# Sums of squares in one block behind two slabs of a linear, instead of a piece behind each chunk

## What is computed

```
x = x + gate * rmsnorm(y, g_post)          # y: output of the block before
h = rmsnorm(x, g_pre) * (1 + scale) + shift
next = h @ w_in                            # the next linear
```

## Time and profile before

| | us |
|---|---|
| median of 3 runs | 3676.74 |
| lowest, highest | 3656.36, 3680.42 |
| the profiled execution | 3671.71 |
| its span | 3669.9 |
| TensorE busy | 3312.0 (90%) |
| VectorE busy | 1804.5 (49%) |
| ScalarE busy | 1076.0 (29%) |
| GpSimd busy | 1045.9 (28%) |
| mean granted clock of TensorE | 0.925 of full |

### The profile page before, as it was taken

The page is one execution under the profiler, slowest core; times in us unless marked ns, Lnnn a source line. Parts: engine busy times, 40 slices in busy tenths (PEclk is TensorE's granted clock), DMA queues, the critical chain, the costliest instruction groups (busy, mean ns, idle before and its releaser), DMA issues.

```text
span 3669.9 us, 53161 instructions
## 1 busy us (share of the span) xinstructions
PE 3312.0 (90%) x17596; PEld 2645.3 (72%) x17600; DVE 1804.5 (49%) x3266; ACT 1076.0 (29%) x1919; POOL 1045.9 (28%) x563
## 2 busy tenths in 40 slices
PE   6789699999988898999988898999999678899997
PEld 4756588888876667998966556788778445578876
DVE  4665777753355664422436465433231366744323
ACT  2144232111131553322222132432231034543222
POOL 1111122323213102444423210444444111134443
PEclk9789899999999998999979795999999669999999
DMA  6101234433111001232211100232222100023222
GB/s 236 55 0 53 97 103 142 145 126 98 54 49 40 1 1 58 92 95 92 88 58 61 45 1 3 81 97 91 93 91 92 46 1 1 1 70 96 95 94 80
DMA packets 74335, 258.67 MB, mean 70 GB/s; under 512 B 9456, under 2 KB 12016, under 8 KB 72688
## 3 DMA queue, kind: packets, MB, share of 16 engines
q1 hardware_dynamic: 60256, 205.61, 17.5%
q10 hardware_dynamic: 13968, 51.65, 4.2%
HBM read 253.03 MB, written 2.10 MB: 70 GB/s over the span
## 4 chain that ended last, share of the span: by engine, by line
PE 81%; DVE 6%; issue 6%; ACT 3%; DVEq 1%; ACTq 1%; DMA 1%; SPq 0%; POOL 0%; POOLq 0%; PEldq 0%
PE ps L799 53%; PE ps L777 6%; PE ps L1995 5%; PE ps L2009 3%; PE ps L1190 2%; PE ps L1195 1%; PE ps L423 1%; PE ps L949 1%; PE ps L463 1%; PE ps L2189 1%; PE ps L2157 1%; DVE ps L400 1%; PE ps L2005 1%; PE ps L2151 1%; DVE rot_s L985 1%
## 5 line engine op out<-in xcount | busy, mean ns | idle before, releaser
L745 POOL TENSOR_TENSOR w_lo<-w_raw,w_hi 128x1024 fp32r<-128x1024 f32 (+1 forms) x373 | 918.3, 2465 | 1810.0 <-ACT w_hi L637 1810.0
L637 ACT ACTIVATE w_hi<-w_raw 128x1024 fp32r<-128x1024 f32 (+1 forms) x373 | 386.1, 1039 | 1284.7 <-PE ps L799 1039.5
L799 PE MATMUL ps<-h_hi,w_hi 128*128 128x258 f32 (+2 forms) x1824 | 321.1, 330 | 48.6 <-ACT w_hi L637 44.3
L799 PEld LDWEIGHTS ps<-h_hi,w_hi 128*128 128x128 f32 x1824 | 272.9, 195 | 82.5 <-issue 37.8
L799 PE MATMUL ps<-h_hi,w_lo 128*128 128x258 f32 (+2 forms) x1824 | 308.7, 321 | 0.0
L799 PE MATMUL ps<-h_lo,w_hi 128*128 128x258 f32 (+2 forms) x1824 | 307.9, 321 | 0.0
L799 PEld LDWEIGHTS ps<-h_hi,w_lo 128*128 128x128 f32 x1824 | 265.6, 190 | 27.7
L799 PEld LDWEIGHTS ps<-h_lo,w_hi 128*128 128x128 f32 x1824 | 264.5, 190 | 26.8
L1995 PE MATMUL ps<-keys,qs 128*128 128x256 f32 (+3 forms) x1008 | 225.3, 352 | 54.1 <-POOL qs L1158 48.2
L1995 PEld LDWEIGHTS ps<-keys,qs 128*128 128x128 f32 x1008 | 159.0, 201 | 117.1 <-issue 94.2
L1232 DVE TENSOR_REDUCE nm<-ps 128x1 f32<-128x512 f32 (+5 forms) x304 | 178.5, 587 | 112.1 <-PE ps L1997 51.9
(11 more groups left out here) (307 smaller groups left out, 5295.1 us busy)
## 6 DMA issues: line engine op xcount, KB each, us to landing
w_raw<-in_ffn_in SPq DMA_DIRECT2D x176, 512.0 KB, 3.6
mod_row<-in_w_mod_rows ACTq DMA_DIRECT2D x80, 512.0 KB, 4.5
w_raw<-in_ffn_out SPq DMA_DIRECT2D x64, 512.0 KB, 3.7
w_raw<-in_ev_in SPq DMA_DIRECT2D x26, 512.0 KB, 3.7
w_raw<-in_ffn_out SPq DMA_DIRECT2D x32, 384.0 KB, 3.1
w_raw<-in_od_in SPq DMA_DIRECT2D x21, 512.0 KB, 3.6
mod_ring<-in_w_mod SPq DMA_DIRECT2D x8, 1024.0 KB, 13.1
w_raw<-in_wo_in SPq DMA_DIRECT2D x12, 512.0 KB, 3.6
```

The costliest lines, as they stand in the source:

```text
L637: act.activation(k.w_hi[:, s, 0:self.KT * P], k.w_raw[:, s, 0:self.KT * P], ACT.Copy).then_inc(k.sems["w_hi_ready"], 1)
L745: ins = pool.tensor_tensor(k.w_lo[:, s, 0:self.KT * P], k.w_raw[:, s, 0:self.KT * P], k.w_hi[:, s, 0:self.KT * P].bitcast(F32), ALU.subtract)
L799: ins = pe.matmul(k.ps[:, 2 * s + g, 0:t1 - t0], w[:, s, c * P:(c + 1) * P], h[:, c, t0:t1], start=(n == 0), stop=(n == len(parts) - 1))
```

## The change

The sums of squares of all 8 chunks stand in one block behind the last matmul of the first two slabs. `n_sq` has 8 buffers instead of two, and the wait of ScalarE on `sq_used` and that semaphore are gone. `n_t` moves to another address, to make room. The number of instructions that compute is the same on every engine.

```diff
@@ class Gate
-        self.b = {... ("gate_x", DC), ("sq_ready", DC), ("sq_used", DC - 1))}
+        self.b = {... ("gate_x", DC), ("sq_ready", DC))}
@@ def pe_squares(self, pe, c):
         pe.wait_ge(k.sems["sq_ready"], self.b["sq_ready"] + c + 1)
         for i in range(self.T // P):
-            ins = pe.matmul(k.ps[:, 6, i:i + 1], k.n_sq[:, c % 2, i * P:(i + 1) * P], ...)
-        ins.then_inc(k.sems["sq_used"] if c < DC - 1 else k.sems["sums_ready"], 1)
+            ins = pe.matmul(k.ps[:, 6, i:i + 1], k.n_sq[:, c, i * P:(i + 1) * P], ...)
+        if c == DC - 1:
+            ins.then_inc(k.sems["sums_ready"], 1)
@@ def scalar(self, act, chain):
             self.pre.act_hi(act, c)
-            if c >= 2:
-
-                act.wait_ge(k.sems["sq_used"], b["sq_used"] + c - 1)
-            act.activation(k.n_sq[:, c % 2, :T], k.x[:, c, :T], ACT.Square).then_inc(k.sems["sq_ready"], 1)
+            act.activation(k.n_sq[:, c, :T], k.x[:, c, :T], ACT.Square).then_inc(k.sems["sq_ready"], 1)
@@ Linear.tensor, the first two slabs behind a Gate
             for c in range(K):
                 order += [hi_in(c), (0, 0, c), (0, 2, c), (1, 0, c), (1, 2, c)]
-                if isinstance(a, Gate):
-                    order.append(lambda c=c: a.pe_squares(pe, c))
                 order += [lo_in(c), (0, 1, c), (1, 1, c)]
             if isinstance(a, Gate):
+                order += [lambda c=c: a.pe_squares(pe, c) for c in range(K)]
                 order.append(lambda: self.norm.pe_spread(pe))
@@ memory
-    k.n_sq = at("n_sq", [P, 2, TOK], F32, A)
-    k.n_t = at("n_t", [P, 2, TOK], F32, A + 6144)
+    k.n_sq = at("n_sq", [P, DC, TOK], F32, A)
+    k.n_t = at("n_t", [P, 2, TOK], F32, A + 24576)
```

More of the change, by code:

```diff
@@ L448, in __init__ @@
         kit.stages[-2].feed()
-        self.b = {n: kit.reserve(n, c) for n, c in (("sums_ready", 1), ("std_ready", 1), ("rstd_ready", 1), ("rstd_spread", 1), ("gate_t", DC), ("gate_x", DC), ("sq_ready", DC), ("sq_used", DC - 1))}
+        self.b = {n: kit.reserve(n, c) for n, c in (("sums_ready", 1), ("std_ready", 1), ("rstd_ready", 1), ("rstd_spread", 1), ("gate_t", DC), ("gate_x", DC), ("sq_ready", DC))}
         self.pre = Pre(kit, norm_cols, shift, groups, hi, lo)
@@ L462, in pe_squares @@
         for i in range(self.T // P):
-            ins = pe.matmul(k.ps[:, 6, i:i + 1], k.n_sq[:, c % 2, i * P:(i + 1) * P], k.ones[:, 0:1], start=(c == 0 and i == 0), stop=(c == DC - 1), skip_group_check=True)
-        ins.then_inc(k.sems["sq_used"] if c < DC - 1 else k.sems["sums_ready"], 1)
+            ins = pe.matmul(k.ps[:, 6, i:i + 1], k.n_sq[:, c, i * P:(i + 1) * P], k.ones[:, 0:1], start=(c == 0 and i == 0), stop=(c == DC - 1), skip_group_check=True)
+        if c == DC - 1:
+            ins.then_inc(k.sems["sums_ready"], 1)
     def scalar(self, act, chain):
```

## The result

| | before | after |
|---|---|---|
| median, us | 3674.23 (4 runs) | 3712.78 (4 runs) |
| lowest, highest | 3656.36, 3680.42 | 3711.64, 3717.33 |
| the profiled execution, span | 3671.71, 3669.9 | 3717.33, 3715.5 |
| mean granted clock | 0.925 | 0.914 |

The change makes the kernel slower: ratio 1.0115, 95% interval 1.0079 to 1.0152. The ratio is formed from all executions; the quotient of the two medians is 1.0105. The forecast was 3712 us (3692 to 3729). The profiled execution of after is the slowest of its four, so the two traces differ by 45.6 us where the medians differ by 38.5.

A forecast was written before the change was run, and what follows sets the result against it. TensorE was taken as the bound, by only 0.27 us per chunk at G1. Slabs and blocks +34.7, spreads +4.6 and restarts +0.7 made +40.0 on the profiled 3671.7: 3712 us, range 3692 to 3729.

The forecast's parts named there:

- End of the slabs: First two slabs at G1 to G4: end 2.8, 2.7, 8.1 and 8.5 us before the old sums' end, 22.1 together.
- The sum: Whole kernel: 34.7 for slabs and blocks, 4.6 for spreads, 0.7 for restarts, +40.0 us on the profiled 3671.7.
- The block: Squares behind the slabs: full clock for 3.5 us, then half; 17.6 us for 96, 10.8 for 64, 56.8 in all.
- The rule weighed against it: In the four blocks, the skill's rule that gapless work keeps full clock: 37.4 us instead of 56.8; the forecast rejected it.
- The spreads: Behind each block, spreads start at half clock: +1.4 us at G1 and G2, +0.9 at G3 and G4, +4.6 together.
- The restart: The third slab's first matmuls behind the spread run more at half clock: +0.7 us, between 0 and +3.
- The other edits: ScalarE's missing wait, the other engines' work and the new addresses: no cost or gain beyond that counted in the loop's end.
- Rival 1: In the four blocks, full clock is kept to the end: +15.3 us, 3687 us; chance 0.09.
- rival 2: The loop can't keep full clock and TensorE enters the block at half: 3726 to 3742 us; chance 0.08.
- rival 3: In the four blocks, squares are cheaper alone, gaining below 0.069 us each; at 0.030, 3659 us; chance 0.03.
- rival 4: No effect: squares stay hidden, or gains at G3 and G4 balance the loss: 3665 to 3680 us; chance 0.02.

The follow-up runs named there:

- experiments 2 to 4: The changed kernel with the block at G3 and G4 only, at G1 and G2 only, or done twice: ratios to before 1.0005, 1.0095 and 1.0309.
- experiment 4: The changed kernel with every block of squares done twice, only the second pass signalling: 3780.03 us, 1.0309 of before.
- experiment 5: The changed kernel with 160 unused 512-column float32r matmuls among the squares in the blocks: 3726.37 us, 1.0161 of before.
- experiment 1: The changed kernel with the squares back between the chunks, keeping eight buffers, new addresses and no wait: 3665.54 us, 0.9992 of before.
- experiment 3: The changed kernel with the block at G1 and G2 only, squares between the chunks elsewhere: 3698.89 us, 1.0095 of before.

## Why the forecast was right, step by step

- *End of the slabs.* It holds to 0.1 us. From the second h_hi to the block's first weight load, which is where the slabs end, after takes 22.53, 22.54, 15.09 and 14.92 us at G1 to G4. Before took 25.33, 25.16, 23.12 and 23.54 to the end of the sums: 22.1 us less together, as forecast. The loops kept VectorE's pace, 3.21 and 2.14 us per chunk. That they do so at full clock, which the forecast assumed, held too: the clock was up by 451, 1069, 1475 and 1891.5, in each loop's first chunks. One reading was too wide: before, TensorE stood at half clock at G3 and G4 in the windows of the earlier trace rows, but from 1449.5 and 1862.5 on it had full clock. The sum doesn't use this, since it goes by the ends of the sums.
- *The block.* 16.2, 16.3, 9.5 and 11.4 us, 53.4 in all where the forecast had 56.8. The half-clock price, 0.2135 from start to start, holds. The full-clock price is 0.112, and the prediction's own rows say so (1.35/12 is 0.1125 and 3.65/32 is 0.114, not 0.117); this makes about 1 us of the 3.4. The rest is when the clock falls: 3.5 us after the block's start was taken, and it fell after 4.8, 4.7, 4.7 and 2.9. The mean of two blocks was a thin basis; its spread of +-1 us was inside the range. In the eight further blocks of experiments 2 to 4 the clock fell too, after 2.5 to 5.3 us.
- *The rule weighed against it.* Had the clock stayed full the blocks would have been 37.4 us long by the prediction's price. Measured 53.4, with TensorE busy in every window. The Trainium skill, TensorE: Matmul & The Clock Gate ("Why this matters for your kernels"), asks only to keep TensorE busy and free of idle gaps between bursts of matmuls. Here that was not enough to hold the clock: by experiment 4 a longer block doesn't bring it back, and by experiment 5 wide matmuls in between keep it.
- *The spreads.* 2.93, 2.93, 2.08 and 2.08 us, the +4.6 of the forecast.
- *The restart.* Mis-sized: +0.7 was taken within 0 to 3. The clock rose 5.2, 6.2, 6.1 and 3.2 us after the third slab's first matmul, where it was 2.8, 3.9, 5.3 and 3.0 before; 5.7 us more at half clock lose some 2.8. At G1 the first 16 matmuls take 5.41 us instead of 4.34.
- *The other edits.* Costed at nothing; experiment 1 shows nothing in its medians.
- *The sum.* Blocks 3.4 under, restarts 2.1 over: -22.1 + 53.4 + 4.6 + 2.8 gives +38.7, and the medians differ by 38.5. That it meets the medians to 0.2 us is luck, since before's four executions alone span 24; so is it that the forecast, 3712, meets the median of 3712.78: the blocks came out shorter and the restarts longer, and it was added to the profiled execution, not to the median. Of the 45.6 us between the two profiled executions, 7.3 are neither at the places nor in the restarts (10.1 - 2.8). Traces scatter by as much where no edit reaches: the stretch from the third slab of G4 to the end takes 1793.3 us before and 1796.5 after, but 1776.6 in experiments 2 and 3 and 1798.9 in experiment 5, with a granted clock of 0.92 in the short ones and 0.91 in the others.
- *Rival 1* (full clock) falls with the windows and experiment 4, *rival 2* with the loops' clock, *rival 3* with 0.112 as the price at full clock against its break-even of 0.069, *rival 4* with the result itself and experiment 3.

One thing stays open. Before spreads from 3652 to 3682 over all its executions, after from 3712 to 3717 in four. In the trace of before the clock rose some 15 us into the loops of G3 and G4, in that of after within 4 to 6 us. This moment varies between executions of the same order: at G2, which is alike in experiments 1 and 2, the clock was up 10.2 us after the first h_hi in the one trace and 4.1 in the other, and the place took 37.1 and 34.3 us. So what the change gains at G3 and G4 will vary too. No run here held it fixed.

## What to carry over

Ask of work that is moved not only how long it is, but what covers it where it goes and what clock it will have there: 320 records of one-column matmuls made the slabs 22.1 us longer between wide ones, only 5.4 of them at G1 and G2, and took 53.4 us in blocks of their own, 32.5 of them at G1 and G2. A block of narrow matmuls is best made short by turning the operands round, before its place in the order is worth a thought. Where a loop will be paced by another engine once the work is out of it, as at G1 and G2, most of the work's time there was covered, and moving it behind the loop mostly costs.

## What the hardware showed that was not expected

- Blocks of nothing but one-column float32 matmuls let the clock fall after 2.9 to 4.8 us in after, though the engine is 100% busy, and 36 us of them in one piece don't bring it back (experiment 4). With wide float32r matmuls in half of the time it stayed full for the whole block (experiment 5).
- A reciprocal on VectorE takes 4.95 us for 768 float32 columns and 3.35 for 512, some 6.5 ns a column, five times an addition of the same tile (0.95).
- An addition on GpSimd, 2.05 us, stretched VectorE's addition beside it from 0.95 to 2.58 us, and so the chunk from 3.21 to 4.83.
